# Feed-forwards: the product of gate and up turned by VectorE and ScalarE in place of TensorE

## What is computed

```python
def rms_norm(x, g):
    xf = x.astype(jnp.float32)
    y = xf * lax.rsqrt(jnp.mean(xf * xf, axis=-1, keepdims=True) + RMS_EPS)
    return (y * g.astype(jnp.float32)).astype(x.dtype)

def swiglu(x, w_gate, w_up, w_down):
    return (jax.nn.silu(x @ w_gate) * (x @ w_up)) @ w_down
...
        h = h + 0.5 * swiglu(rms_norm(h, norm_ffn[layer, 0]), ffn_w_gate[layer, 0],
                             ffn_w_up[layer, 0], ffn_w_down[layer, 0])
```

## Time and profile before

| What | Value |
|---|---|
| median of 3 runs | 1973.66 us (1972.43 to 1973.99) |
| profiled execution, in all | 1972.11 us |
| its span, first to last instruction | 1970.3 us |
| instructions | 26042 |
| TensorE busy | 1960.1 us, 99% |
| VectorE busy | 1140.4 us, 58% |
| ScalarE busy | 1013.8 us, 51% |
| GpSimd busy | 68.9 us, 3% |
| mean DMA rate | 172 GB/s |

### The profile page before, as it was taken

The page is one execution under the profiler, slowest core; times in us unless marked ns, Lnnn a source line. Parts: engine busy times, 40 slices in busy tenths (PEclk is TensorE's granted clock), DMA queues, the critical chain, the costliest instruction groups (busy, mean ns, idle before and its releaser), DMA issues.

```text
span 1970.3 us, 26042 instructions
## 1 busy us (share of the span) xinstructions
PE 1960.1 (99%) x9838; PEld 1652.5 (84%) x9838; DVE 1140.4 (58%) x1641; ACT 1013.8 (51%) x1587; POOL 68.9 (3%) x77
## 2 busy tenths in 40 slices
PE   9999999999999999999999999999999999999999
PEld 7888988888888898888888898888888888888887
DVE  6555656556555566555655566655576555876553
ACT  6444555445444665444544447544476444755442
POOL 0100300000000000000000000000010000200000
PEclk9999999999999999999999999999999999999999
DMA  9665436554655426555555434555456553306550
GB/s 342 208 205 171 150 108 214 192 192 132 225 183 177 140 80 210 192 192 171 195 181 186 161 132 144 198 192 192 171 168 231 185 187 126 108 23 213 192 192 22
DMA packets 241048, 338.91 MB, mean 172 GB/s; under 512 B 5727, under 2 KB 206350, under 8 KB 240830
## 3 DMA queue, kind: packets, MB, share of 16 engines
q1 hardware_dynamic: 239710, 335.84, 50.3%
q0 software_dynamic: 496, 1.23, 0.2%
q10 hardware_dynamic: 752, 0.61, 0.1%
HBM read 336.61 MB, written 1.05 MB: 171 GB/s over the span
## 4 chain that ended last, share of the span: by engine, by line
PE 96%; ACT 2%; DVE 1%; DMA 1%; issue 0%; SPq 0%; POOL 0%; ACTq 0%
PE A L535 11%; PE A L537 11%; PE A L536 11%; PE G L535 10%; PE G L537 10%; PE G L536 10%; PE X L535 8%; PE X L537 8%; PE X L536 8%; PE A L1226 1%; PE A L904 1%; PE G L964 1%; PE X L964 1%; PE X L1210 1%; PE G L1238 1%; PE A L1654 0%
## 5 line engine op out<-in xcount | busy, mean ns | idle before, releaser
L496 DVE TENSOR_TENSOR wl<-raw,wh 128x1024 fp32r<-128x1024 f32 (+1 forms) x553 | 655.1, 1224 | 169.8 <-ACT wh L487 169.1
L487 ACT ACTIVATE wh<-raw 128x1024 fp32r<-128x1024 f32 (+1 forms) x553 | 561.6, 1057 | 142.3 <-PE A L537 102.1
L535 PE MATMUL G<-wh,xh 128*128 128x512 f32 (+1 forms) x814 | 322.1, 396 | 0.7 <-ACT arena L2228 0.4
L537 PE MATMUL G<-wh,xl 128*128 128x512 f32 (+1 forms) x814 | 317.3, 390 | 0.0
L536 PE MATMUL G<-wl,xh 128*128 128x512 f32 (+1 forms) x814 | 316.4, 389 | 0.0
L535 PE MATMUL X<-wh,xh 128*128 128x512 f32 x672 | 265.8, 396 | 0.0
L537 PE MATMUL X<-wh,xl 128*128 128x512 f32 x672 | 262.4, 390 | 0.0
L536 PE MATMUL X<-wl,xh 128*128 128x512 f32 x672 | 261.7, 389 | 0.0
L537 PEld LDWEIGHTS G<-wh,xl 128*128 128x128 f32 x814 | 152.8, 188 | 32.3
L535 PEld LDWEIGHTS G<-wh,xh 128*128 128x128 f32 x814 | 152.9, 188 | 31.6 <-DVE xl L2400 0.8
L536 PEld LDWEIGHTS G<-wl,xh 128*128 128x128 f32 x814 | 153.1, 188 | 29.9
(11 more groups left out here) (485 smaller groups left out, 2641.9 us busy)
## 6 DMA issues: line engine op xcount, KB each, us to landing
raw<-in_ffn_w_in SPq DMA_DIRECT2D x88, 1024.0 KB, 6.6
raw<-in_ffn_w_down SPq DMA_DIRECT2D x44, 1024.0 KB, 6.6
raw<-in_ffn_w_out SPq DMA_DIRECT2D x44, 1024.0 KB, 7.1
raw<-in_ffn_w_gate SPq DMA_DIRECT2D x42, 1024.0 KB, 5.3
raw<-in_ffn_w_up SPq DMA_DIRECT2D x42, 1024.0 KB, 7.4
raw<-in_a_w_in SPq DMA_DIRECT2D x12, 1024.0 KB, 5.9
raw<-in_ab_w_in SPq DMA_DIRECT2D x8, 1024.0 KB, 6.8
raw<-in_kv_w SPq DMA_DIRECT2D x6, 1024.0 KB, 6.2
```

The source lines that it names most:

```text
L487: nc.scalar.activation(hi, r, ACT.Copy).then_inc(hi_done[u], 1)
L496: nc.vector.tensor_tensor(lo, r, hi.bitcast(F32), ALU.subtract).then_inc(lo_done[u], 1)
L535: nc.tensor.matmul(o, sh, rh, start=start, stop=False)
L537: return nc.tensor.matmul(o, sl, rh, start=False, stop=stop)
```

## The change

For ten of the eleven blocks of each feed-forward, TensorE no longer transposes the hidden tile. VectorE runs one transpose over the whole 128 x 512 tile, which turns each 32 x 32 square in itself (`turn_squares`, into `squares_t`). ScalarE then copies the squares to where they belong: what stands in square row i, column j goes from partitions 32i to partitions 32j. One copy takes that square of all four 128-wide pieces, so there are 16 copies of 32 partitions x 4 x 32 elements (`move_squares`, into `hid_t`). The high part and the low part are then one instruction of 128 x 512 each, from SBUF, in place of two of 128 x 256 from PSUM. ScalarE does this ahead of the down weights of the step; VectorE takes the low part ahead of them too. The last block of each feed-forward keeps the transposes of TensorE (`turn_last_hid`, `last_hid_hi`, `last_hid_lo`). `gate_up(b, 0)` now waits for `hid_done` of block b - 2.

```diff
-        hid = cut(work, 4 * S, 2, S)
+        hid, squares_t, hid_t = cut(work, 4 * S, 2, S), cut(work, 2 * S, 2 * S), cut(work, 6 * S, 2 * S)
...
+                    if b > 1 and half == 0:
+                        pe.wait_ge(hid_done, 2 * (FFN_BLOCKS * f + b - 2) + 2 + at)
...
-                def turn_hid(b, turn=None):
-                    at = 0 if turn is None else 4 * turn
+                def turn_last_hid():
+                    b = FFN_BLOCKS - 1
                     for t in range(NT):
...
                 def step(b, turn=None):
                     gate_up(b, 0, turn)
-                    turn_hid(b - 1, turn)
                     gate_up(b, 1, turn)
                     down(b - 1, turn)
...
                 gate_up(end, 0)
-                turn_hid(end - 1)
                 gate_up(end, 1)
...
+                def move_squares(b, turn=None):
+
+                    at = 0 if turn is None else 4 * turn
+                    n = 2 * (FFN_BLOCKS * f + b) + 2
+                    if b:
+                        act.wait_ge(hidl_done, n - 2 + at)
+                    act.wait_ge(hid_turned, n + at)
+                    for i in range(4):
+                        for j in range(4):
+                            src = squares_t[32 * i:32 * i + 32, :].rearrange("p (a n) -> p a n", n=P)[:, :, 32 * j:32 * j + 32]
+                            dst = hid_t[32 * j:32 * j + 32, :].rearrange("p (a n) -> p a n", n=P)[:, :, 32 * i:32 * i + 32]
+                            last = A_(dst, src, ACT.Copy)
+                    last.then_inc(hid_moved, 2)
+
                 def hid_hi(b, turn=None):
                     at = 0 if turn is None else 4 * turn
-                    for t in range(NT):
-                        act.wait_ge(hid_turned, 2 * (FFN_BLOCKS * f + b) + t + 1 + at)
-                        A_(hidh[:, b % 2, t * S:(t + 1) * S], GB[b % 2][t][:, 0:S], ACT.Copy).then_inc(hidh_done, 1)
+                    act.wait_ge(hid_moved, 2 * ((FFN_BLOCKS - 1) * f + b) + 2 + at)
+                    A_(hidh[:, b % 2, :], hid_t, ACT.Copy).then_inc(hidh_done, 2)
...
+                    move_squares(b - 1, turn)
+                    hid_hi(b - 1, turn)
                     for half in (0, 1):
                         prepare_hi(base + 2 * b + half, 2, turn)
-                    hid_hi(b - 1, turn)
...
+                def turn_squares(b, turn=None):
+
+                    at = 0 if turn is None else 4 * turn
+                    dve.wait_ge(hid_done, 2 * (FFN_BLOCKS * f + b) + 2 + at)
+                    V.transpose(squares_t, hid.rearrange("p t s -> p (t s)")).then_inc(hid_turned, 2)
+
                 def hid_lo(b, turn=None):
                     at = 0 if turn is None else 4 * turn
+                    dve.wait_ge(hidh_done, 2 * (FFN_BLOCKS * f + b) + 2 + at)
+                    V.tensor_tensor(hidl[:, b % 2, :], hid_t, hidh[:, b % 2, :].bitcast(F32), ALU.subtract
+                                    ).then_inc(hidl_done, 2)
...
                     hidden(b - 1, turn)
+                    turn_squares(b - 1, turn)
                     for half in downs:
...
+                    hid_lo(b - 1, turn)
                     for half in (0, 1):
                         prepare_lo(base + 2 * b + half, 2, turn)
-                    hid_lo(b - 1, turn)
```

More of the change, by code:

```diff
@@ L375, in blocks_program @@
         xhi_done, xlo_done, acc_done = sem("xhi_done"), sem("xlo_done"), sem("acc_done")
-        silu_ready, hid_done = sem("silu_ready"), sem("hid_done")
+        silu_ready, hid_done, hid_moved = sem("silu_ready"), sem("hid_done"), sem("hid_moved")
         hid_turned, hidh_done, hidl_done = sem("hid_turned"), sem("hidh_done"), sem("hidl_done")
@@ L956, in gate_up @@
                     last.then_inc(used[1], 1)
-                def turn_hid(b, turn=None):
-                    at = 0 if turn is None else 4 * turn
+                def turn_last_hid():
+                    b = FFN_BLOCKS - 1
                     for t in range(NT):
-                        pe.wait_ge(hid_done, 2 * (FFN_BLOCKS * f + b) + t + 1 + at)
+                        pe.wait_ge(hid_done, 2 * (FFN_BLOCKS * f + b) + t + 1)
                         for j in range(2):
@@ L1024, in ffn @@
                     if q == 3:
-                        turn_hid(end)
+                        turn_last_hid()
                     for j in range(2):
@@ L1794, in gate, with last_hid_hi @@
                         A_(silu[:, t, :], GB[b % 2][t][:, 0:S], ACT.Silu, scale=rstd[:, t:t + 1]).then_inc(silu_ready, 1)
+                def last_hid_hi():
+                    b = FFN_BLOCKS - 1
+                    for t in range(NT):
+                        act.wait_ge(hid_turned, 2 * (FFN_BLOCKS * f + b) + t + 1)
+                        A_(hidh[:, b % 2, t * S:(t + 1) * S], GB[b % 2][t][:, 0:S], ACT.Copy).then_inc(hidh_done, 1)
+                def move_squares(b, turn=None):
[10 more added lines that the diff above has]
+                    last.then_inc(hid_moved, 2)
                 def hid_hi(b, turn=None):
                     at = 0 if turn is None else 4 * turn
-                    for t in range(NT):
-                        act.wait_ge(hid_turned, 2 * (FFN_BLOCKS * f + b) + t + 1 + at)
-                        A_(hidh[:, b % 2, t * S:(t + 1) * S], GB[b % 2][t][:, 0:S], ACT.Copy).then_inc(hidh_done, 1)
+                    act.wait_ge(hid_moved, 2 * ((FFN_BLOCKS - 1) * f + b) + 2 + at)
+                    A_(hidh[:, b % 2, :], hid_t, ACT.Copy).then_inc(hidh_done, 2)
                 def step(b, turn=None, split=(), downs=()):
@@ L1861, in ffn @@
                     prep(name, FT + 1, (0, 1))
-                hid_hi(FFN_BLOCKS - 1)
+                last_hid_hi()
             def start(name):
@@ L2452, in hidden, with last_hid_lo @@
                         V.tensor_tensor(hid[:, t, :], GB[b % 2][t][:, S:2 * S], silu[:, t, :], ALU.mult).then_inc(hid_done, 1)
+                def turn_squares(b, turn=None):
+                    at = 0 if turn is None else 4 * turn
+                    dve.wait_ge(hid_done, 2 * (FFN_BLOCKS * f + b) + 2 + at)
+                    V.transpose(squares_t, hid.rearrange("p t s -> p (t s)")).then_inc(hid_turned, 2)
                 def hid_lo(b, turn=None):
                     at = 0 if turn is None else 4 * turn
+                    dve.wait_ge(hidh_done, 2 * (FFN_BLOCKS * f + b) + 2 + at)
+                    V.tensor_tensor(hidl[:, b % 2, :], hid_t, hidh[:, b % 2, :].bitcast(F32), ALU.subtract
+                                    ).then_inc(hidl_done, 2)
+                def last_hid_lo():
+                    b = FFN_BLOCKS - 1
                     for t in range(NT):
-                        dve.wait_ge(hidh_done, 2 * (FFN_BLOCKS * f + b) + t + 1 + at)
+                        dve.wait_ge(hidh_done, 2 * (FFN_BLOCKS * f + b) + t + 1)
                         part = slice(t * S, (t + 1) * S)
@@ L2524, in ffn @@
                     prep(name, FT + 1, (0, 1))
-                hid_lo(FFN_BLOCKS - 1)
+                last_hid_lo()
                 if name == "ffn0":
```

## The result

| | before | with the change |
|---|---|---|
| median | 1973.31 us (4 runs) | 1940.61 us (1939.95 to 1943.03, 4 runs) |
| ratio | | 0.9837, 95% interval 0.982 to 0.9854 |
| span of the profiled execution | 1970.3 us | 1938.0 us |

It is 32.7 us faster, 1.6%. The forecast was 1936.5 with a range of 1932 to 1945.

The account below looks back on a forecast made before the run. TensorE, busy 99% of the span, was taken as the bound. 80 turns at 0.48 us give 38.4, less 1.2 of first-block waits is 37.2, so the median of 1973 or so becomes 1936.5 us, range 1932 to 1945.

Parts of the forecast that it names:

- losses in the first blocks: TensorE's waits in the first block of ffn0, ffn4 and ffn6: 0 to 0.1, 0.6 and 0.4, taken as 1.2 us.
- the cover: In steady blocks, TensorE's 16.3 us hide ScalarE's copies, which uncovered would cost 3.2 us per block, 256 in all.
- TensorE is the bound and a turn costs 0.48 us: TensorE, busy 99%, sets the time; without its turn a block goes from 16.81 to 16.33 us.
- the busy time of 87 us: Rival: TensorE's whole busy time of the removed transposes, 87 us, goes, giving 1886.6; chance 0.01.
- Ten blocks of eleven, 80 turns, 38.4 us: Ten of eleven blocks in each of 8 feed-forwards lose TensorE's turn: 80 x 0.48 = 38.4 us.
- 16 copies at 0.20 us: ScalarE's copies overlap and start 0.20 us apart, adding 3.2 us per block; 0.32 if each drains first.
- rival 2: ScalarE copies cost 0.32 to 0.50 us, first blocks' down products wait: 1938.4 (only ffn0) to 1952; chance 0.13.
- the first case: The forecast itself: TensorE stays the bound, small waits in first blocks only; 1936.5, own range 1932 to 1942, chance 0.79.
- the second case: Another name for rival 2: dearer copies between partitions on ScalarE, 1938.4 to 1952; chance 0.13.
- The transpose delays weights in ffn4 and ffn6 by 0.6 and 0.4: In these first blocks VectorE's transpose, taken as 0.69 us, delays low parts of weights; TensorE loses 0.6 and 0.4 us.
- The down weights behind the copies, the extra wait for `hid_done`: Down weights queued behind ScalarE's copies are wanted a block later; TensorE's added semaphore was set about a block earlier: nothing.
- Slower only from 0.586 us per copy: Rival: ScalarE bounds the block beyond 0.556 us per copy, no gain from 0.586; at 0.64, 2042 us; chance 0.04.

Follow-up runs that it names:

- e1: Changed kernel with the two loops of `move_squares` swapped, so four copies in a row keep the destination partitions and change the source; 1941.42 us.
- e3: Changed kernel with all 16 copies moving data by one quadrant, four in a row with the same source and destination (wrong values); 1938.52 us.
- e2: Changed kernel with each of the 16 copies writing the partitions it reads, four in a row on one quadrant (wrong values); 1937.63 us.
- e4: Changed kernel with one 128x512 copy that moves nothing between partitions in place of the 16 (wrong values); median 1935.99 us, ratio 0.981.
- e7: Changed kernel with VectorE's final norm in ffn4 put behind step 2 in place of ahead of it; median 1937.51 us, ratio 0.9822.
- e9: Changed kernel with 48 smaller copies of the same data, ordered so that the pair of partitions changes at every copy; 2258.76 us.
- e8: Changed kernel with TensorE turning the first block of ffn0, ffn4 and ffn6 as before the change; median 1935.96 us, ratio 0.9814.
- e5: Changed kernel with 48 smaller copies of the same data, the three of each square in a row; 1965.1 us.

## Why the prediction was right, and where it was off

The forecast, 1936.5, was 4.1 us too low: the bound, the number of turns and their price were right, and they are nearly all of the change. The losses in the first blocks were put at 1.2 us and measured 5.6. By one of its own signs it was wrong: it named copies that start more than 0.3 us apart, and they start 0.32 apart. In steady blocks the cover, which had been worked out, hid that; in ffn0 and ffn4 it showed, and the time stayed within the range because the range reached to 1945. So the measured time does not bear out the copies' price.

- **TensorE is the bound and a turn costs 0.48 us.** Right: 16.81 became 16.32, 0.49 per turn; the busy time of 87 us was not what went.
- **Ten blocks of eleven, 80 turns, 38.4 us.** Right: 39.5.
- **16 copies at 0.20 us.** This is the term that was off. They start 0.32 us apart, the upper of the two rows' numbers. I had named it ("0.32, if each has to drain before the next") and chosen the lower, because the copies wait for nothing between them. They don't wait for a semaphore, but they change partitions, and e1 to e3 show that this decides. In the steady block it made no difference, since the cover was as large as worked out. In ffn0 it made 1.9 us in place of 0 to 0.1, which is what rival 2 gave for 0.32. The measured 1940.6 lies in the first case's own range (1932 to 1942), and also 2.2 us above the 1938.4 that the second gave for 0.32; by the mechanism it is the lower end of the second case, to which as a whole 0.13 had been given. The Trainium skill's figure (VectorE: DVE Perf Modes, section on the TRN2 errata), 350 cycles for a copy of 128 elements or 0.29 us as an estimate, was nearer to the 0.32 us measured than my choice; but e2 shows copies of the same size about 0.20 us apart, so it isn't the size of the copy that decides.
- **Rival 2: at 0.32 only ffn0 waits.** Wrong for ffn4, 1.6 us. I checked the hidden tile's way to the down products (late by nothing) and not what is queued behind its low part on VectorE: down weights, 2.5 us of norm, and only then the weights of the next block. e4 and e7 show it from both sides: without the copies the wait goes, and without the norm in that place it goes too.
- **The transpose delays weights in ffn4 and ffn6 by 0.6 and 0.4.** Right, 0.59 and 0.44, and nothing in the ordinary five. The transpose is 0.71, near the 0.69 taken, not 0.42.
- **The down weights behind the copies, the extra wait for `hid_done`.** Costed at nothing, and TensorE has no idle time in steady blocks.
- **Slower only from 0.586 us per copy.** Not reached. e9 shows that the copies do become the bound, through the ring of ScalarE and VectorE; the point where it happens is worked out as about 0.53 us each in place of 0.556.

The sum, put right: 39.5 less the 5.6 in the three feed-forwards is 33.9, which would have given 1939.8. The 0.8 that is left to the measured 1940.6 is within what the wait for `x` and the stage `kv` differ by between executions.

## What to carry to other kernels

Work may be moved from a full engine to one with idle time almost for free in a steady loop, as long as the new engine's queue and every ring through it stay shorter than a block, even if the move takes ten times as long there (0.49 us on TensorE against 5.1 + 0.7 here); count what is queued behind it on the new engine, and look at the first turn of the loop by itself, since there the distance to the consumer is shortest. If some turns have no slack, leave those on the old engine (e8). Group small ScalarE copies so that neighbours have the same source and destination partitions.

## What the runs showed of the hardware that was not expected

- ScalarE's copies overlap only while source and destination start at the same partitions as in the copy before. Sixteen copies of 32 x 128: 3.64 us with the pair kept for four in a row, 5.1 with one side changing each time. Forty-eight small copies of the same data: 8.05 against 11.88 us. Moving between quadrants (groups of 32 partitions) costs nothing else (3.66 against 3.64).
- TensorE ran at half speed behind some of its waits: behind 2.0 us for `x` in e1, at those of 4.9, 3.5 and 2.8 us in e5, and not behind the 1.9 us in ffn0 of the changed kernel. In e9, whose mean granted clock was 0.956, this is the resumption after 3.11 us of idle time:

```profile
640.43 0.66 PE L535 MATMUL A<-mh,hidh 128*128 128x512 f32 x1 [3.11 <-DVE hidl L2484]
640.88 0.63 PE L536 MATMUL A<-ml,hidh 128*128 128x512 f32 x1
...
644.18 0.39 PE L535 MATMUL A<-mh,hidh 128*128 128x512 f32 x1
644.40 0.39 PE L536 MATMUL A<-ml,hidh 128*128 128x512 f32 x1
```

  Matmuls start 0.43 us apart until 643.9, then 0.23 again; the window from 640 to 648 has a granted clock of 0.79, a part of it at 1.2 GHz and the rest at 2.4. These matmuls ended some 1.6 us later for it (8 x 0.20), but the block did not: TensorE's next wait was 1.52 us in place of 3.11, and the block was 19.73 us as the one after it, since the ring sets its length. In e5, where TensorE is the bound, such stretches do lengthen the time. Not every wait of that length did it: at 679.89, after the same 3.11 us, the clock stayed at 2.4 GHz. What decides between them stays open.
